# Moving the channel transform and the radix-4 level of a Fourier mixer into the input projection

## The reference

```
h = rmsnorm(x)
z = h @ w_in                       # 512 Fourier columns, 512 Q, 128 K, 128 V
f = Re(fft2 over (positions, 128 channels)) per group of 128 channels; f = f @ w_fourier[g]
a = banded attention (8 heads, 2 kv heads, |i-j| <= 128, sink, T5 bias)
x = x + concat(f, a) @ w_out
x = x + expert_choice_moe(rmsnorm(x))      # 16 SwiGLU experts
y = rmsnorm(x)
```

## Time and profile before

| | us |
|---|---|
| Median of 3 runs | 3038.07 |
| Lowest and highest | 3037.46, 3040.09 |
| The profiled execution | 3041.85 |
| Its span | 3040.1 |
| TensorE busy | 2741.2 |
| VectorE busy | 1444.7 |
| ScalarE busy | 1200.4 |
| GpSimd busy | 365.7 |

### The profile page before, as it was taken

How to read it: one execution, slowest core, us unless ns; L and a number is a source line. 1 busy time by engine, 2 the same in 40 slices (tenths; PEclk the granted TensorE clock), 3 DMA queues, 4 the chain that set the end, 5 groups by cost and what they waited for, 6 DMA issues and landing times. The chain is left out here.

```text
span 3040.1 us, 41988 instructions
## 1 busy us (share of the span) xinstructions
PE 2741.2 (90%) x15311; PEld 2445.9 (80%) x15311; DVE 1444.7 (48%) x2859; ACT 1200.4 (39%) x2121; POOL 365.7 (12%) x289
## 2 busy tenths in 40 slices
PE   7999979639999997199999999999999999999980
PEld 5888867628888886199999999999999999999980
DVE  4122155536666664744444445444544444444425
ACT  3122134436666563034433443343434334433325
POOL 0000000012222220001101110111111011101110
PEclk9999989869999998599999999999999999999995
DMA  5121131374545443135535444554454445535437
GB/s 171 73 96 73 48 121 62 111 190 130 138 128 141 133 127 128 38 136 157 153 133 177 132 156 154 154 157 141 160 161 132 162 148 155 156 132 178 132 94 293
DMA packets 238810, 414.86 MB, mean 136 GB/s; under 512 B 11867, under 2 KB 84476, under 8 KB 238732
## 3 DMA queue, kind: packets, MB, share of 16 engines
q1 hardware_dynamic: 213068, 344.57, 34.8%
q0 software_dynamic: 25664, 69.28, 9.5%
HBM read 326.59 MB, written 87.22 MB: 136 GB/s over the span
## 5 line engine op out<-in xcount | busy, mean ns | idle before, releaser
L1183 DVE TENSOR_TENSOR we_lo<-we_raw,we_hi 128x1024 fp32r<-128x1024 f32 x384 | 467.2, 1224 | 603.7 <-ACT we_hi L1178 603.2
L117 PE MATMUL p_psum<-p_xT_hi,we_hi 128*128 128x384 f32 x2048 | 693.1, 338 | 0.0
L119 PE MATMUL p_psum<-p_xT_hi,we_lo 128*128 128x384 f32 x2048 | 685.4, 335 | 0.0
L118 PE MATMUL p_psum<-p_xT_lo,we_hi 128*128 128x384 f32 x2048 | 685.2, 335 | 0.0
L1178 ACT ACTIVATE we_hi<-we_raw 128x1024 fp32r<-128x1024 f32 x384 | 401.2, 1057 | 5.9 <-DMA we_raw<-w_gate 5.8
L118 PEld LDWEIGHTS p_psum<-p_xT_lo,we_hi 128*128 128x128 f32 x2048 | 384.8, 188 | 0.6
L117 PEld LDWEIGHTS p_psum<-p_xT_hi,we_hi 128*128 128x128 f32 x2048 | 384.5, 188 | 0.6
L119 PEld LDWEIGHTS p_psum<-p_xT_hi,we_lo 128*128 128x128 f32 x2048 | 384.5, 188 | 0.0
L117 PE MATMUL p_psum<-we_hi,p_hid_hi 128*128 128x512 f32 x768 | 300.3, 391 | 0.0
L119 PE MATMUL p_psum<-we_hi,p_hid_lo 128*128 128x512 f32 x768 | 299.0, 389 | 0.0
L118 PE MATMUL p_psum<-we_lo,p_hid_hi 128*128 128x512 f32 x768 | 298.9, 389 | 0.0
(11 more groups left out here) (214 smaller groups left out, 4184.9 us busy)
## 6 DMA issues: line engine op xcount, KB each, us to landing
we_raw<-w_gate SPq DMA_DIRECT2D x32, 2048.0 KB, 7.8
we_raw<-w_up SPq DMA_DIRECT2D x32, 2048.0 KB, 8.1
we_raw<-w_down SPq DMA_DIRECT2D x32, 2048.0 KB, 8.8
zT<-p_z SPq DMA_DIRECT2D x54, 256.0 KB, 2.0
p_x<-x POOLq DMA_DIRECT2D x6, 2048.0 KB, 8.1
p_q_raw<-zT SPq DMA_DIRECT2D x48, 256.0 KB, 4.7
p_x<-x SPq DMA_DIRECT2D x24, 512.0 KB, 5.9
h<-p_h SPq DMA_DIRECT2D x24, 512.0 KB, 2.6
```

The costliest lines, as they stand in the source:

```text
L117: pe.matmul(out, lhi, rhi, start=first, stop=False)
L118: pe.matmul(out, lhi, rlo, start=False, stop=False)
L119: return pe.matmul(out, llo, rhi, start=False, stop=last)
L1183: dve.tensor_tensor(self.lo[:, n % self.HL, ks], self.raw[:, n % self.RAW, ks], self.hi[:, n % self.HL, ks].bitcast(F32), ALU.subtract).th ...
```

## The change

- The bias rows are one product with 8 rows as its result, one evacuation from 8 partitions, and a store whose source repeats each of the 8 rows 128 times. SP issues it after the second piece of w_in.
- A chunk of the projection now holds four tiles of 128 tokens, one of each quarter of a sequence: chunks 0 to 3 are the long sequence, 4 and 5 the short. Its x comes in two loads. SP holds w_in back until the first half of the first x has come.
- w_in comes in five pieces of 256 columns (1 MB in runs of 1 KB). A group waits only for its own piece. The splits of pieces 1 to 4 follow the first chunk's h_hi and h_lo.
- The four Fourier groups come first, are split straight from PSUM and are not stored. Four products with the channel matrix (12 matmuls of width 256 each) stand between the other groups. ScalarE copies two of the results, VectorE does the other two and the four turns, and SP stores the turns (2 MB a chunk) in `turned`. The squares of the next chunk stand behind the third Fourier split.
- GpSimd loads the first four turns for the next stage while the projection still runs.
- The Fourier stage is left with the position units. Buffers are a ring of four units; each unit loads its turn from `turned` beside its table.
- The long and the short result have tensors of their own, and nothing waits for the store of the long one.
- At unit 16 of 24 SP issues the first loads of attention into buffers of the new class `AttentionInputs`; f is loaded once its store has landed. `attend_and_mix` keeps its own order from the third Q and K block on.

```diff
+    def product(self, pe, bank):
+        pe.wait_ge(self.rb_in, 32)
+        pe.matmul(bank[0:NH, :NREL], self.rb[:, :], self.buckets[:, :], start=True, stop=True).then_inc(self.mm, 1)
...
+        sp.wait_ge(self.out, 1)
+        sp.dma_start(toeplitz.rearrange("h (p n) -> h p n", n=NREL),
+                     self.rows[:, :].unsqueeze(1).to_broadcast([NH, P, NREL])).then_inc(self.stored, 16)
...
+            bias_rows.load(sp, rel_bias, bucket_rows)
+            sp.dma_start(cc, chan_cos).then_inc(chan_in, 16)
+            sp.dma_start(cs, chan_sin).then_inc(chan_in, 16)
+            sp.dma_start(wf, w_fourier.rearrange("g p c -> p g c")).then_inc(chan_in, 16)
             sp.dma_start(ident[:, :], ident_d).then_inc(const_in, 16)
             sp.dma_start(g_col[:, :], g_mix_cols).then_inc(const_in, 16)
-            bias_rows.load(sp, rel_bias, bucket_rows)
+            sp.wait_ge(x_in[0], 16)
             for i in range(WP):
                 if i >= 2:
                     sp.wait_ge(w_lo_done, i - 1)
...
+                sp.dma_start(w_raw[:, i % 2], w_v[:, :, piece(i)]).then_inc((w_in0, w_in1)[i % 2], 16)
+                if i == 1:
+                    bias_rows.store(sp, toeplitz)
...
+                for r in range(RADIX):
+                    sp.wait_ge(turn_done, c * 6 + (1, 3, 4, 6)[r])
+                    sp.dma_start(turned[c, r], turn(r)).then_inc(turn_stored, 16)
...
+                for half in range(2):
+                    tiles = slice(half * CH // 2, (half + 1) * CH // 2)
+                    pool.dma_start(x_sb[:, tiles], x_v[s][:, tiles]).then_inc(x_in[half], 16)
...
+            pool.wait_ge(t_done, NCH * KT)
+            pool.wait_ge(turn_stored, 16 * RADIX * LONG)
+            for i in range(CH):
+                pool.dma_start(x_sb[:, i], turned[i % LONG, i // LONG]).then_inc(first_in[i], 16)
...
+                if isinstance(c, int) and c == 0:
+                    for i in range(1, WP):
+                        split_hi(act, i)
+                for g in range(NF):
                     if g == 0:
-                        act.wait_ge(stored, c * (16 * GRP))
-                        act.wait_ge(vt_done, c)
+                        act.wait_ge(uv_mm, c * RADIX)
                     act.wait_ge(m_done, c * GRP + (g + 1))
-                    act.activation(z_sb[:, g], ps[:, 4 + g % 4], ACT.Copy, scale=scale_of(g)).then_inc(z_act, 1)
-
+                    act.activation(zf_hi[:, g], ps[:, bank_of(g)], ACT.Copy).then_inc(zf_hi_done, 1)
+                    if g == 2 and not last:
+                        squares(c + 1)
+                evacuate(c, V)
+                uv_out(c, 0)
+                evacuate(c, V + 2)
+                uv_out(c, 2)
+                evacuate(c, V + 4)
...
+            squares(0)
+            split_hi(act, 0)
+            act.wait_ge(ab_mm, 1)
+            act.activation(ab_hi[:, :].rearrange("p g c -> p (g c)"), ab_psum, ACT.Copy).then_inc(ab_hi_done, 1)
...
+                near, far = quarter(QORDER[i - 1]), quarter(QORDER[i])
+                dve.wait_ge(uv_act, c * 2 + (i // 2 + 1))
+                dve.wait_ge(uv_mm, c * RADIX + (i + 1))
+                dve.tensor_tensor(far, near, pair(i), ALU.subtract).then_inc(uv_dve, 1)
+                dve.tensor_tensor(near, near, pair(i), ALU.add).then_inc(uv_dve, 1)
...
+                dve.tensor_tensor(turn(0), a, d_, ALU.add).then_inc(turn_done, 1)
...
+                    dve.tensor_tensor(re_w, re_b, im_d, one).then_inc(turn_done, 1)
+                    dve.tensor_tensor(im_w, im_b, re_d, two).then_inc(turn_done, 1)
+                    if r == 1:
+                        dve.tensor_tensor(turn(2), a, d_, ALU.subtract).then_inc(turn_done, 1)
...
+                evacuate(c, V + 1)
+                half_turn(c, 1)
+                dve.wait_ge(vt_done, c + 1)
+                dve.tensor_copy(v_sb[:, :].rearrange("p j n -> p (j n)"), ps[:, bank_of(V)]).then_inc(v_done, 1)
+                evacuate(c, V + 3)
+                half_turn(c, 3)
+                turns(c)
+                evacuate(c, K)
...
+            bias_rows.evacuate(dve, ps[:, bank_of(1)])
+            normalise(0)
+            split_lo(dve, 0)
...
+                elif g == 2:
+                    pe.wait_ge(ab_lo_done, 1)
+                elif g == V:
+                    pe.wait_ge(zf_lo_done, c * NF + 1)
+                elif V < g < V + 4:
+                    pe.wait_ge(zf_lo_done, c * NF + (g - V + 1))
+                elif g == V + 4:
+                    pe.wait_ge(v_done, c + 1)
+                elif g == K:
+                    pe.wait_ge(z_dve, c * 3 + 1)
+                pe.wait_ge(w_lo_done, needs(g))
...
+                if i == 0:
+                    pe.wait_ge(zf_lo_done, c * NF + NF)
+                elif i == 2:
+                    pe.wait_ge(uv_act, c * 2 + 1)
+                elif i == 3:
+                    pe.wait_ge(uv_dve, c * 4 + 2)
...
+                for g in range(FG):
+                    out = pair(i)[:, g * 2 * FD:(g + 1) * 2 * FD]
+                    last = three_pass(pe, out, zf_hi[:, g, tokens], zf_lo[:, g, tokens], ab_hi[:, g], ab_lo[:, g], True, True)
+                last.then_inc(uv_mm, 1)
...
+                for g in range(V + 1):
+                    group(c, g)
+                channels(c, 0)
+                group(c, V + 1)
+                channels(c, 1)
...
+                group(c, V + 2)
+                channels(c, 2)
+                group(c, V + 3)
+                channels(c, 3)
+                group(c, V + 4)
+                group(c, K)
...
+            for i, (n, r, s) in enumerate(units):
+                if i >= RING:
+                    sp.wait_ge(w_lo_done, i - RING + 1)
+                    if (n, r, s) == (1, 0, 0):
+                        sp.wait_ge(turn_stored, 16 * RADIX * (TT // RADIX))
+                        sp.wait_ge(z_stored, 16 * (IN_W // P - FG) * (TT // RADIX))
+                        inputs.load_early(sp)
+                    sp.dma_start(w[:, i % RING], turned[firsts[n] + s, r]).then_inc(w_in[i % RING], 16)
+                if i >= RING:
+                    sp.wait_ge(tab_lo_done, i - RING + 1)
+                sp.dma_start(tab[:, i % RING, :, :width(n)], pos_tables[n][r, :, s]).then_inc(tab_in[i % RING], 16)
+            sp.wait_ge(stored, 16 * FG)
+            for t in range(2):
+                inputs.load_f(sp, t)
 
...
+            for i, (n, r, s) in enumerate(units):
+                if i >= RING:
+                    act.wait_ge(f_mm, i - RING + 1)
+                if i < RING:
+                    act.wait_ge(first_in[i], 16)
+                else:
+                    act.wait_ge(w_in[i % RING], 16 * (i // RING))
+                act.activation(w_hi[:, i % RING], w[:, i % RING], ACT.Copy).then_inc(w_hi_done, 1)
+                act.wait_ge(tab_in[i % RING], 16 * (i // RING + 1))
+                act.activation(tab_hi[:, i % RING, :, :width(n)], tab[:, i % RING, :, :width(n)], ACT.Copy).then_inc(tab_hi_done, 1)
+                if s == 1 and i > 1:
+                    evacuate(*units[i - 2][:2], i - 2)
+            evacuate(*units[-1][:2], len(units) - 1)
...
+        attn_sink, ident_d, toeplitz, g_ffn, w_router = self.given
+        sp.dma_start(self.ident[:, :], ident_d).then_inc(self.const_in, 16)
+        sp.dma_start(self.sink[:, :], attn_sink.partition_broadcast(P)).then_inc(self.const_in, 16)
+        self.load_qk(sp, 0)
+
+        skew = toeplitz[:, P - 1:P - 1 + P * (NREL - 1)].rearrange("h (p n) -> p h n", n=NREL - 1)
+        sp.dma_start(self.bias[:, :], skew[:, :, :BAND]).then_inc(self.bias_in, 16)
+        self.load_qk(sp, 1)
+        self.load_v(sp, 0)
+        for i in range(2):
+            self.w_out.load(sp, i)
+        self.load_v(sp, 1)
+        self.load_x(sp, 0)
+        sp.dma_start(self.gain[:, :], g_ffn.partition_broadcast(P)).then_inc(self.late_in, 16)
+        sp.dma_start(self.wr[:, :], w_router.rearrange("(k p) e -> p k e", p=P)).then_inc(self.late_in, 16)
...
```

More of the change, by code:

```diff
@@ new lines, in bank_of, with pair, piece, needs @@
+        def bank_of(g):
+            return 4 + g % 4
+        def pair(i):
+            first = 2 if i % 2 == 0 else 0
+            return ps[:, first:first + 2].rearrange("p b c -> p (b c)")
+        def piece(i):
+            return slice(PIECES[i] * P, PIECES[i] * P + PW)
+        def needs(g):
+            return next(i for i in range(WP) if piece(i).start <= cols_of(g).start < piece(i).stop) + 1
+        def split_hi(act, i):
+            act.wait_ge((w_in0, w_in1)[i % 2], 16 * (i // 2 + 1))
+            act.activation(w_hi[:, :, piece(i)], w_raw[:, i % 2], ACT.Copy).then_inc(w_hi_done, 1)
@@ L299, in _ @@
[L299 to L308 removed]
+                if isinstance(c, int) and c == 0:
+                    for i in range(1, WP):
+                        split_lo(dve, i)
@@ new lines, in body @@
+                for g in range(NF):
+                    if g == 0:
+                        dve.wait_ge(uv_mm, c * RADIX)
```

(32 more changed lines are left out.)

552 lines of the change are left out of this document (218 added, 334 removed).

## The result

The changed kernel takes 2995.01 us (median of 4 runs, 2991.59 to 2996.5) against 3038.14 for the kernel before on the same chip: a ratio of 0.9851, with a 95% interval of 0.9838 to 0.9865. It is faster by 43 us; I had forecast 80, and the time lies 5 us above the upper end of my range. The profiled executions, 3041.85 and 2991.59, are 50.3 apart; on their scale the sum had promised 80.5.

What follows compares the result with a forecast made beforehand. TensorE was taken to bound the kernel, busy 90% of the span, with recoverable waits around the Fourier stage and attention's head. Terms -14.9 +34.8 +8 -38.9 -8.4 -37.1 -24 sum to -80.5, giving 2957.6 us, range 2940 to 2990.

Steps and rivals of the forecast that it cites:

- the bias store: +8, between 0 and 33: First projection chunk: the 2 MB Toeplitz store ahead of weight pieces 2 to 4 stalls TensorE, +8 us.
- three cases: Bias store's stall: none at the earlier store's queue cost; 16.5 us on half the queues; 32.5 if source partitions set pace.
- The bias store holds back the weights: Rival, first projection chunk: stall of 16.5 for 8 gives 2966, 32.5 if the source sets the pace 2982; chance 0.2.
- Channel products: Projection: six chunks of 16 three-pass products on TensorE's path add 34.8 us; their evacuations stay off it.
- the rival of chunk stalls: Projection: a stall of 1.5 to 3 us in each chunk behind the fourth split, 2967 to 2976; chance 0.07.
- Border: Projection to position stage: 51.3 becomes 12.4, -38.9 us; first table queues behind 2.25 MB of stores; bounds 8 and 18.
- Long position phase: Long sequence's position units: 97.8 becomes 89.4, -8.4 us, as waits for w_lo at turn borders go.
- The rival that the loads bound it: Long position phase: a unit's two loads run one after the other, 7.0 for 5.45 us, +24, 2982; chance 0.06.
- Short phase: Short sequence's position units: 61.6 becomes 24.5, -37.1 us, as z loads, splits, uv products and ScalarE's store wait go.
- Head of attention: Start of attention: 71.4 becomes 47.4, -24 us, from early loads; w_out through two buffers late next; bounds -12 and -32.
- The rival without a gain: Head of attention: w_out's two buffers pace it as before, 24 come back as 4, 2978; chance 0.06.
- Slower: First chunk, before the fifth group: store ending after 116.5, 102 us of queue, outweighs 88.5 gained elsewhere; chance 0.04.

Runs made afterwards that it cites:

- the run with the store last: Changed kernel with only the bias store moved in SyncE's queue, from behind piece 1 to behind the last weight piece: 2965.23 us, ratio 0.9753.
- the run with the delayed stores: Bias store behind the last weight piece, plus GpSimd's four stores of the long sequence's result made to wait for the last position table: 2968.17 us, ratio 0.9759.

## Why the prediction was wrong, and where it was right

The direction was right; the failing step is the term *the bias store: +8, between 0 and 33*.

*The bias store.* It cost 29.6 us as the sum counts it, the 417.7 of the projection less 353.3 and 34.8, and 27.4 by the run with the store last. I had three cases, and the one with the source's partitions as the pace was the right one. It put piece 2's landing at 60.5, and it came at 60.3; it had 14.9 us from there to the fifth group, and it was 14.4; it gave 32.5 in all. That the landing fits to 0.2 us is in part luck: I had the store run from 14.5 for 46 us, it ran from 16.2 to 56.8, and the half of piece 2 that was still out needed the 3.5 us behind it. I chose 8, from the row that was nearest in name, a store of the same bytes from 128 partitions, though the source is the very thing that the change alters. My other cases were also too kind: the first gave no stall at all, and with 128 partitions it is 12.2: the store was over at 33.7, but piece 2 came 11.6 us behind it, beside chunk 1's activations, 2 MB that were not in my queue. The rival "The bias store holds back the weights" is what happened, and its port price gave 2982. The 13 us above that are the lines below (8.5), less 2.9 for the store itself, and the profiled executions' places beside their medians (7.1): 3.7 above for the kernel before, 3.4 below for the changed one.

*Start.* First product at 25.70 for 26: the load in halves, the second table load and the order of splits hold. The store last gave 25.47.

*Channel products.* Chunks of 65.4 as worked out, and no wait over 0.3 us in a steady chunk. The half microsecond of cover behind the fourth split was enough; the rival of chunk stalls falls.

*Border.* 13.4 for 12.4, by the mechanism given, stores ahead of the tables. What I took as fixed was the order of those stores, which alone is worth 5 us of wait.

*Long position phase.* 89.2 for 89.4, with a DMA share of 0.77 and no wait for w_lo. The rival that the loads bound it falls.

*Short phase.* 28.8 for 24.5. I had named its covers, attention's loads and the 4 MB of stores, and took both as free. The stores cost 3 to 5 us, as the run with the delayed stores shows, the loads between nothing and 2.

*Head of attention.* 49.6 for 47.4, and 21 to 23 us for the early loads when they are taken back. The rival without a gain falls. That w_out through two buffers would be late next was right; a third buffer is worth 8 us.

*Rest.* 1.5 us more in 2365, not followed up.

*A wrong sum.* The time outside the matmuls is not 129 us in the stretches that I named: by the earlier trace rows it is 103. No term rests on it.

*Slower.* It needed a store that holds the queue for 102 us. It held piece 2 until 60.3, and 43 us of gain were left.

## What to carry to other kernels

Price a DMA by the partitions that it reads or writes, not by its bytes: a store fed from eight neighbouring partitions moved some 50 GB/s, from eight spread ones 98, from single ones 29. When the change alters the very property that makes a transfer fast, the old transfer's row is one end of the range, not its middle. And what nobody needs soon is issued behind what somebody waits for. That one line was worth 30 us here, more than any repair of the store itself, and a second queue was no way around it.

## What the runs showed of the hardware

- A slow DMA on half of the engines (share 0.50) held another queue's loads for 38.7 us: pieces issued 1.3 us later from SyncE waited for a store issued from GpSimd. From 26 to 46 us packet went for packet, 160 of the store's 6,132 bytes and 160 of the pieces' 1 KB.
- In one queue too the store held only the engines that it ran on: half of the packets of pieces 2 and 3 had gone by 45 us, the other half began at 56.0, with the store over at 56.8.
- Eight DMAs from one partition each took nearly all engines (0.90) and ran at little over half the pace of one DMA from eight (29 for 52 GB/s); SyncE was held for 50.9 us in issuing them.
- Eight partitions at steps of 16 shortened the wait to 13.1 us, 128 partitions to 12.2. By the bit rule of the Trainium skill, "SBUF — State Buffer" (Door 1: The DMA port swizzle), partitions 0, 16, 32 to 112 reach four ports, not eight, against two for the first eight; the stores' packets, at 98 and 52 GB/s, agree with twice the ports.
- A stall of 26.9 us also cost the clock: TensorE's granted clock was 0.50 to 0.52 of full speed, its 1.2 GHz level, in the two stretches of 10 us from 60 to 80 us, and the first products after the stall ran at it; with the store last it was 1.00 in both.
